# Attention's value products of two slots back to back in every second step, where one slot's stood in each step

## The reference, cut to what matters

```python
def attend(q, k, v, scale):
    s = jnp.einsum('bhgqd,bhkd->bhgqk', q, k).astype(jnp.float32) * scale
    p = jax.nn.softmax(s, axis=-1).astype(v.dtype)
    return jnp.einsum('bhgqk,bhkd->bhgqd', p, v)
```

## Time and profile before

| | |
|---|---|
| median of 3 runs | 3692.05 us (3689.9 to 3698.3) |
| the profiled execution: time, span | 3690.47 us, 3688.5 us |
| mean granted TensorE clock, whole span | 0.968 |
| PE busy, DVE busy, ACT busy, POOL busy | 94%, 50%, 36%, 19% |
| attention's slots in the trace | 449 to 953 us |

### The profile page before, as it was taken

One profiled execution on the slowest core, in us unless ns is written; L12 is line 12 of the kernel. 1 busy time (PEld: TensorE's weight loads), 2 busy tenths in 40 slices (PEclk: granted clock), 3 DMA queues, 4 the chain that ended last, 5 costly groups with the idle time before them and its releaser, 6 DMA issues. The chain is left out here.

```text
span 3688.5 us, 40136 instructions
## 1 busy us (share of the span) xinstructions
PE 3471.0 (94%) x15670; PEld 2471.0 (67%) x15670; DVE 1830.5 (50%) x2317; ACT 1332.2 (36%) x2143; POOL 690.2 (19%) x398
## 2 busy tenths in 40 slices
PE   6989799999899999999996989899989899999997
PEld 3655244555688888888886868653344688888886
DVE  3332744433266554554675534476355565444444
ACT  4323344444554333333453223441110443223332
POOL 0000277666332201200211000110000230002001
PEclk8999799999999999999998999998999999999999
DMA  8744532321244333433453211101501343333332
GB/s 336 277 165 122 146 68 58 79 56 45 92 149 136 116 97 97 137 97 97 155 190 126 92 53 40 36 35 58 199 18 52 114 166 97 97 97 120 120 97 97
DMA packets 140528, 408.65 MB, mean 111 GB/s; under 512 B 24621, under 2 KB 41421, under 8 KB 136052
## 3 DMA queue, kind: packets, MB, share of 16 engines
q1 hardware_dynamic: 140340, 406.08, 33.8%
HBM read 344.73 MB, written 61.21 MB: 110 GB/s over the span
## 5 line engine op out<-in xcount | busy, mean ns | idle before, releaser
L1438 ACT ACTIVATE w_high<-w_raw 128x1024 fp32r<-128x1024 f32 x360 | 380.1, 1056 | 579.8 <-PE psum L1414 471.9
L1524 DVE TENSOR_TENSOR w_low<-w_raw,w_high 128x1024 fp32r<-128x1024 f32 x360 | 453.2, 1259 | 119.8 <-ACT w_high L1438 118.8
L1414 PE MATMUL psum<-hid_high,w_high 128*128 128x512 f32 (+1 forms) x1280 | 472.6, 369 | 10.3 <-DVE hid_low L1592 8.7
L1397 PE MATMUL psum<-h_high,w_high 128*128 128x512 f32 (+1 forms) x1280 | 474.7, 371 | 2.1 <-DVE w_low L1524 2.1
L1397 PE MATMUL psum<-h_high,w_low 128*128 128x512 f32 (+1 forms) x1280 | 470.9, 368 | 0.0
L1397 PE MATMUL psum<-h_low,w_high 128*128 128x512 f32 (+1 forms) x1280 | 470.9, 368 | 0.0
L1414 PE MATMUL psum<-hid_low,w_high 128*128 128x512 f32 (+1 forms) x1280 | 470.8, 368 | 0.0
L1414 PE MATMUL psum<-hid_high,w_low 128*128 128x512 f32 (+1 forms) x1280 | 470.8, 368 | 0.0
L1614 POOL TENSOR_TENSOR squares_then_rstd_of_out<-squares_then_rstd_of_out,square_out 128x512 f32<-128x512 f32 (+1 forms) x70 | 102.4, 1464 | 1284.7 <-ACT square_out L1453 1284.1
L1178 POOL TENSOR_TENSOR probs_added<-probs_added,probs_turned 128x1024 f32<-128x1024 f32 x128 | 305.0, 2383 | 66.7 <-ACT probs_turned L1107 62.5
L1146 DVE TENSOR_REDUCE row_max<-psum 128x1 f32<-128x1280 f32 x128 | 190.3, 1491 | 243.6 <-PE psum L1055 147.3
(11 more groups left out here) (406 smaller groups left out, 5385.8 us busy)
## 6 DMA issues: line engine op xcount, KB each, us to landing
w_raw<-in_ff_w_dram SPq DMA_DIRECT2D x320, 512.0 KB, 3.5
ada_ring<-in_ada_w_dram SPq DMA_DIRECT2D x24, 2048.0 KB, 9.5
w_raw<-in_w_out_dram SPq DMA_DIRECT2D x40, 512.0 KB, 3.5
stream_in<-scratch_x SPq DMA_DIRECT2D x32, 256.0 KB, 4.0
scratch_spectra<-spectrum_out SPq DMA_DIRECT2D x32, 256.0 KB, 2.0
filter_ring<-scratch_spectra SPq DMA_DIRECT2D x16, 512.0 KB, 4.8
w_raw<-in_w_hy_dram SPq DMA_DIRECT2D x12, 512.0 KB, 3.5
scratch_hyena<-hy_conv SPq DMA_DIRECT2D x12, 512.0 KB
```

What stands on the lines that cost most here:

```text
L1397: mm = pe.matmul(bank[:, 0:n], x[:, i % SLOTS, k, :], y[:, k, a:a + n], start=(k == 0 and m == 0), stop=(k == KT - 1 and m == 2))
L1414: mm = pe.matmul(bank[:, 0:n], x[:, i % SLOTS, 2 * k + half, :], y[:, k, 0:n], start=(k == 0 and m == 0), stop=(k == HT - 1 and m == 2))
L1438: act.activation(w_hi[:, i % SLOTS], raw[:, i % 2], ACT.Copy).then_inc(w_rounded, 1)
L1524: dve.tensor_tensor(w_lo[:, i % SLOTS], raw[:, i % 2], w_hi[:, i % SLOTS], ALU.subtract).then_inc(w_split, 1)
```

## The change

In even steps the values of slots i-2 and i-1 are issued one after the other; in odd steps none. Even slots keep their step, odd slots are taken one step earlier. All 176 slots are covered, since every unit ends in an odd slot. ACT, DVE, POOL and SP keep their code and order.

```diff
                     if 0 <= i < N:
                         scores_of(i)
-                    if 0 <= i - LAG < N:
-                        values_of(i - LAG)
+                    if i % 2 == 0 and 2 <= i <= N:
+                        values_of(i - 2)
+                        values_of(i - 1)
                     if i in rank_at:
                         leading_scores(rank_at[i])
```

## The result

The changed kernel takes 3705.95 us (median of 7, 3699.61 to 3714.84) against 3692.34 (7 runs, 3687.84 to 3698.3): a ratio of 1.0043, 95% interval 1.003 to 1.0057. It is slower by 13.6 us. The forecast was 3708 in a range of 3694 to 3722.

What follows compares the result with a forecast made beforehand. TensorE's issue order was taken to bound attention (TensorE busy 94% of the span). Stalls and savings, priced pair of steps by pair of steps, summed to +15.8, say +16 us: 3708, range 3694 to 3722.

Steps and rivals of the forecast that it cites:

- What joining saves: Two slots' values of 512 queries issued together on TensorE: 0.15 us saved once per joined pair, 1.87 us in all.
- second kind: Heads whose leading scores have the scores' form: step of 3.21 us before, pair of steps 6.42 to 6.51, +0.09.
- The rival that joining gives nothing: In the joined values, the exit is paid between the slots too: +13 us, 3721; chance 0.12.
- the one that it saves twice as much: In the joined values, the saving is double: -13 us, 3695, no measurable change; chance 0.15.
- What the odd step loses: Odd leading product waits for the reduce, 2.19 or 2.44 us after the even one: TensorE idle 0.50 or 0.34.
- the reduce does not hold the odd step: Rival for the odd step's leading product: only the savings are left, -17.6 us, 3674; chance 0.06.
- Two leading products: First-kind pairs of steps (step of 2.70 us before) with leading scores in both: 5.40 to 5.75 us, +0.35.
- pair 3: Pair of heads computing pair 4's leading scores in first-kind steps: pair of steps 5.52 to 6.06 us, +0.54.
- offsets 18 and 20 together: Late steps: offset 18 about +0.37 us in the first kind, +0.12 in the second; offset 20 +0.83 and +0.79.
- The clock: Rival: new gaps lower TensorE's granted clock in attention; each tenth at half clock adds up to 50 us, 3758; chance 0.05.
- The pairs of steps without leading scores: Pair 7 from offset 8: joining saves 0.35 us, an exponential wait takes back 0.25, so -0.10, six times.
- POOL and the ring: POOL does 4.8 us of work in a 5.75 us pair of steps, so the ring does not hold ACT.

Runs made afterwards that it cites:

- the fourth experiment: Kernel before the change, with values joined only in the steps of offset 6 and 8 of each pair of heads: 3688.95 us against 3690.54, ratio 0.9989.
- The short reduce: Changed kernel, row maximum over 512 of 1280 scores, exponential of a quarter of the scores (output not the reference's): 3673.05 us against 3690.54 for the kernel before.
- the leading product between the values: Changed kernel with the even step's leading product put between its two slots of values: 3688.28 us against 3690.54 for the kernel before, ratio 0.9995.
- the last experiment: Kernel before, with the reduce split in three parts and values joined only in pairs of steps that had shown a gain: 3683.38 us against 3694.72, ratio 0.9971.
- second profile: The changed kernel run once more, unaltered, for its own noise: 3713.32 us against 3692.8 for the kernel before, ratio 1.0056.

## Why the prediction was right

- *The bound.* TensorE's issue order sets the stage: every lost or saved fraction of a step appeared in the stage's length.
- *What joining saves.* 0.15 for the exit, and 0.10 each for the entry and exit between full forms that fall away in the second kind: measured alone at offsets 6 and 8, -0.15 and -0.35, in the changed kernel and in the fourth experiment. That the row had 256 queries and stood beside sums did not matter. The rival that joining gives nothing is out, and so is the one that it saves twice as much.
- *What the odd step loses.* The distance of 2.19 and 2.44 us was 2.20 and 2.44. The short reduce took the loss away, and the leading product between the values did too, each by its own way of making the reduce fit. The count of waits was 58 for some 56. The rival "the reduce does not hold the odd step" is out in the changed kernel; its consequence, a faster kernel, is what the short reduce gave. That its median, 3673.05, agrees with the rival's 3674 is luck: the rival's -17.6 us are of the stage, which gave -11.7.
- *Pairs of steps.* Two leading products: +0.35 forecast, +0.36 measured; second kind +0.09, measured 0.07 to 0.14; pair 3 +0.54, measured 0.56 to 0.61; offsets 18 and 20 together +1.20, measured 1.26 to 1.30, and +0.91, measured 1.00 to 1.04.
- *The clock.* Its mean over the stage stayed at 0.99; the rival is out.

One price was right for a reason that the forecast did not have, and one was wrong. In pairs of the second kind the odd leading product there follows scores of its own form, so by the forecast's own rule it needed no entry, 0.60 and not the 0.70 of the sum. It takes 0.68 (722.90 to 723.58), since it has waited; where it does not wait, in the last experiment, it takes 0.59 (719.97 to 720.56). The agreement of these pairs is luck in this term: with 0.60 in all 28 places the sum would have been about 3 us lower, near 13. The wrong one is offset 8 of pair 3, priced at -0.15: its odd leading product is of the second kind, and it gave -0.35.

The stretch of offsets 18 to 20, TensorE with the exponential that the next scores wait for:

```profile
571.19 0.50 PE L1014 MATMUL psum<-q_other,k_high 128*128 128x512 f32 x1
...
572.04 1.08 ACT L1108 ACTIVATE probs_turned<-psum 128x512 f32<-128x512 f32 x2 [1.92 <-PE psum L1017]
572.69 0.39 PE L1014 MATMUL psum<-q_other,k_high 128*128 128x256 f32 x1 [0.31 <-ACT probs_turned L1108]
```

1.50 us from one slot's first scores to the next one's, forecast 1.51.

The sum was 15.8 us and the stage grew by 19.0; the terms that were too small:

- *The first joined block ran at the slow clock*, about 1.1 us. I had put the first pairs of steps at the price of all others. TensorE stands at the lower level, 1.2 GHz, from before the first slot in either kernel; at offset 2 of pair 0 the changed kernel lost 1.42 and, in its second profile, 1.50, for 0.37 elsewhere. The row: eight records at 3.6 us from start to start, for 1.86.

```profile
460.41 3.68 PE L1027 MATMUL psum<-probs_turned,v_pair 128*64 128x512 f32 x8
...
464.02 0.79 PE L1057 MATMUL psum<-k_high,q_leading 64*128 64x512 f32 x1
```

  The clock rose 9.4 us after the stage's start before and 11.6 us after it in the changed kernel (in these rows by stretch the granted clock is the 0.50 behind the last bracket):

```profile
449.33:458.70 9.37, 9.37 (x24) 4.45 (x23) 3.99 (x3) 3.58 (x6) 3.66 (x2) 0.50 0.49 114
453.12:464.70 11.58, 11.58 (x29) 5.24 (x27) 3.98 (x3) 3.58 (x6) 4.71 (x2) 0.50 0.39 89
```

  By estimate, 2.2 us more at half the clock are worth 1.1. The profile of the fourth experiment, whose code up to there is that of before, had 14.0 us at 0.50 and +2.05 at this offset; the other kernels had between -0.24 and +0.95. So how much of the 1.1 is the change's is open.
- *The pairs of steps without leading scores* (pair 7 from offset 8): -0.10 each forecast, about 0.0 measured, 0.6 us in all. The wait is as forecast (1.74), 1.73 from the odd scores (965.05) to the next (966.78), but the scores that waited then take 1.61 to the values: their first product again takes 0.35 in place of 0.24. I had priced an entry only where the form changes.

```profile
965.05 0.50 PE L1011 MATMUL psum<-q_leading,k_high 96*128 96x512 f32 x1
...
966.13 1.23 ACT L1108 ACTIVATE probs_turned<-psum 128x512 f32<-128x512 f32 x2 [2.25 <-PE psum L1017]
...
966.78 0.51 PE L1011 MATMUL psum<-q_leading,k_high 96*128 96x512 f32 x1
967.13 0.39 PE L1012 MATMUL psum<-q_other,k_high 96*128 96x512 f32 x1
...
968.39 0.65 PE L1027 MATMUL psum<-probs_turned,v_pair 128*64 128x512 f32 x2
```

- The same first product after the waits at offsets 18 to 20 makes 0.1 for each of pairs 0 to 6, about 0.7 us; the end of the stage, put at 0, came out 0.4 longer; and the first kind's ordinary pairs were 0.01 to 0.02 above the forecast. With these the stage is accounted for.

*POOL and the ring* were forecast not to hold ACT. They do, 19 times and 30.9 us, since the exponentials now come two close together; it reached nobody. "The ring does not hold ACT" was wrong as said and right for the time.

That 3705.95 lies nearer to the forecast than the stage does is partly chance: the stage alone would have given 3711, and the second measurement gave 3713.32.

## What to carry to other kernels

Before moving work together, look at what it kept apart: here the values were the distance between two products that share one area, and TensorE paid 0.3 to 0.5 us each time for the reduce of 1.49 us that had been covered. Price a moved step pair by pair, with the earliest possible start of each instruction from both sides (its engine's order, and the chain that gives its buffer back), and keep the edit where that price is negative: the same edit on chosen steps, with the area given back in parts, was faster than before where the whole one was slower. Start times of one repeated instruction, subtracted between two traces, resolve 0.02 us where medians of this kernel resolve some 7.

## What the runs showed of the hardware

- Leaving the form with half the columns cost 0.15 us and entering it 0.10 (0.33 for 0.24 from start to start), the same in all eight pairs of heads. A first product after a wait costs the same 0.10, though its form is that of the one before: 966.78 to 967.13, and 0.68 for 0.59 in leading products of the second kind. The two did not add where both fell together: leading products of the first kind took 0.54 with the wait (562.11 to 562.65) as without it.
- A reduce from PSUM of 1280, 512 and 256 elements a partition took 1491, 685 to 692 and 414 ns. A straight line through these has about 0.15 us that are there whatever the length, and a reduce in three parts is 0.29 us longer in sum; from first start to last end it was 0.13 longer, 1.62 us.
- The stage began at 442.9 to 454.1 us in eleven profiled executions, and what follows it took between 7 us less and 7 us more than in the profile of the kernel before, though this code is the same in all of them. The stage itself repeated within 0.1 us in the changed kernel's two profiles. So execution times of this kernel move by several us for reasons outside the changed code.
